# The front end of a streaming-encoder layer in another order, with its input projection as products of split halves

## What is computed

```python
h = layer_norm(x)                                   # input norm
proj = h @ w_in + b_in                              # 1024 -> 2304 columns, split into 8 parts
y_lru = rg_lru(lru_x, ...) * gelu(lru_gate)         # 512 + 512 columns
y_swa = sliding_window_gqa(sq, sk, sv, ...)         # 256 + 128 + 128 columns
y_sb  = stick_breaking(bq, bk, bv)                  # 256 + 256 + 256 columns, 4 heads
y = concat(group_rms(y_lru), group_rms(y_swa), group_rms(y_sb))
h = layer_norm(alpha * h + y @ w_out + b_out)
h = layer_norm(alpha * h + moe_ffn(h))              # top 4 of 32 experts
```

## Time and profile before

| | |
|---|---|
| median of 3 runs | 1484.73 us (1483.04 to 1486.56) |
| the profiled execution, its time | 1485.46 us |
| its span, first to last instruction | 1483.8 us |
| end of the front end in it | about 309 us |
| granted TensorE clock, mean | 0.989 |
| busy in the span: PE, DVE, ACT, POOL | 96%, 82%, 66%, 34% |
| busy in the first 309 us: PE, DVE, ACT, POOL | 284.2, 150.4, 111.3, 65.1 us |

### The profile page before, as it was taken

One profiled execution on the slowest core, in us unless ns is written; L12 is line 12 of the kernel. 1 busy time (PEld: TensorE's weight loads), 2 busy tenths in 40 slices (PEclk: granted clock), 3 DMA queues, 4 the chain that ended last, 5 costly groups with the idle time before them and its releaser, 6 DMA issues.

```text
span 1483.8 us, 20629 instructions
## 1 busy us (share of the span) xinstructions
PE 1430.4 (96%) x6623; PEld 1121.7 (76%) x6623; DVE 1215.0 (82%) x1002; ACT 975.9 (66%) x710; POOL 501.0 (34%) x309
## 2 busy tenths in 40 slices
PE   7999979998999999999999999999999999999994
PEld 3466548986888888888888888888888888888873
DVE  5533366476999999999999999999999999999985
ACT  2244660165777777777777777777777777777772
POOL 4200124152334333333334334444443333333101
PEclk9999999998999999999999999999999999999998
DMA  8221135469999999999999999999999999999933
GB/s 265 69 61 54 42 121 220 167 251 332 356 380 385 379 379 390 378 377 379 386 377 373 371 382 385 386 382 389 382 375 380 380 377 378 387 373 380 358 130 126
DMA packets 86311, 461.44 MB, mean 311 GB/s; under 512 B 11912, under 2 KB 26506, under 8 KB 37130
## 3 DMA queue, kind: packets, MB, share of 16 engines
q1 hardware_dynamic: 75190, 431.91, 74.0%
q0 software_dynamic: 9648, 26.49, 7.7%
q10 hardware_dynamic: 1444, 2.66, 0.7%
HBM read 443.92 MB, written 25.76 MB: 317 GB/s over the span
## 4 chain that ended last, share of the span: by engine, by line
PE 74%; DVE 1%; DMA 1%; POOL 1%; issue 1%; POOLq 0%; DVEq 0%; ACT 0%; ACTq 0%
PE banks L1737 69%; PE banks L1705 2%; PE banks L1711 2%; DMA acc_dram<-glu_lin 1%; PE banks L1769 1%; POOL sel L1436 1%; PE banks L1832 0%; POOLq L1438 0%; DVE raw L1666 0%; DVEq L1557 0%; DVE raw L1670 0%; PE banks L1699 0%; PE banks L1837 0%; DVE glu_lin L1553 0%; ACT hi L1324 0%
## 5 line engine op out<-in xcount | busy, mean ns | idle before, releaser
L1516 DVE TENSOR_TENSOR lo<-raw,hi 128x2048 fp32r<-128x2048 f32 x384 | 866.8, 2289 | 77.2 <-ACT hi L1324 76.3
L1324 ACT ACTIVATE hi<-raw 128x2048 fp32r<-128x2048 f32 x384 | 733.7, 1920 | 251.3 <-PE banks L1737 251.0
L1737 PE MATMUL banks<-hi,x_hi 128*128 128x512 f32 x1040 | 287.0, 397 | 9.3 <-DVE x_lo L1540 6.9
L1737 PE MATMUL banks<-lo,x_hi 128*128 128x512 f32 x1040 | 280.1, 391 | 0.0
L1737 PE MATMUL banks<-hi,x_lo 128*128 128x512 f32 x1040 | 279.7, 390 | 0.0
L1436 POOL TENSOR_SCALAR sel<-cst,rank_e 128x128 bf16<-128x128 f32 x120 | 219.4, 1840 | 126.8 <-issue 126.8
L1737 PEld LDWEIGHTS banks<-lo,x_hi 128*128 128x128 f32 x1040 | 195.8, 188 | 42.0
L1737 PEld LDWEIGHTS banks<-hi,x_hi 128*128 128x128 f32 x1040 | 191.1, 189 | 48.1 <-issue 11.7
L1737 PEld LDWEIGHTS banks<-hi,x_lo 128*128 128x128 f32 x1040 | 195.8, 188 | 41.6
L1459 POOL DMA_INDIRECT acc_dram<-ye,dst_row x31 | 50.2, 1620 | 363.5 <-ACT ye L1349 363.5
L1737 PE MATMUL banks<-hi,a_hi 128*128 128x512 f32 x496 | 155.7, 395 | 0.0
(11 more groups left out here) (276 smaller groups left out, 1226.1 us busy)
## 6 DMA issues: line engine op xcount, KB each, us to landing
raw<-in_w_exp_in SPq DMA_DIRECT2D x256, 1024.0 KB, 7.6
raw<-in_w_exp_out SPq DMA_DIRECT2D x128, 1024.0 KB, 6.7
raw<-in_w_in SPq DMA_DIRECT2D x9, 1024.0 KB, 7.9
raw<-in_w_out SPq DMA_DIRECT2D x4, 1024.0 KB, 5.0
x<-in_x SPq DMA_DIRECT2D x4, 512.0 KB, 6.0
h_dram<-x SPq DMA_DIRECT2D x4, 512.0 KB, 2.6
bias_in<-bias_dram SPq DMA_DIRECT2D x128, 3.0 KB
raw<-acc_dram SPq DMA_DIRECT2D x4, 512.0 KB, 5.9
```

What stands on the lines that cost most here:

```text
L1324: act.activation(hi[:, c0 % PARTS, :], raw[:, c0 % RAW, :], ACT.Copy).then_inc(hi_done, 1)
L1516: dve.tensor_tensor(lo[:, c0 % PARTS, :], raw[:, c0 % RAW, :], hi[:, c0 % PARTS, :].bitcast(F32), ALU.subtract).then_inc(lo_done, 1)
L1737: last = pe.matmul(psum[:, bank + n, :], s[:, k, :], w[:, at:at + 512], start=(first and m == 0 and new), stop=(closes and m == steps - 1 ...
```

## The change

Six things change, all in the front end.

1. The list starts with the stick-breaking heads: `bq`, `bk`, `bv` come first, the LRU's inputs later, the gates `g` and the window's score products later still. The norm of the stick-breaking group comes first (`NORM_ORDER = [2, 0, 1]`).
2. The input projection is three products of split halves instead of a plain float32 product. ACT makes the high half of the weights (`w_hi`, type float32r), DVE the low half (`w_lo`, the weights minus the high half), half a chunk at a time (`w_part`). The activations are split as well: ACT writes `hT_hi`, POOL subtracts the shift from it (`h_raw`), DVE makes `hT_lo` from the PSUM bank and that (`h_part`). A float32r product is one pass on PE, and there are three of them.
3. The two halves live where `raw` lies: `w_lo` over slots 0 and 1, `w_hi` over slots 2 and 3, so that only two chunks are held (`MIX_RAW = 2`). `hT_lo` lies over `x`, `hT_hi` over `h1T`, so the residual is no longer kept: x is loaded again once all input jobs are done, ACT normalises it (step `res`), and POOL applies gain, shift, alpha and the output bias.
4. `sv` is computed like the other jobs and transposed by a new job `u0`.
5. The window softmax is cut in two steps, `most` (maxima) and `window`; the small LRU constants become a step `lam`.
6. The output projection takes 512 columns at a time, and for the first token tile goes by the groups of channels, in the order of the norms; two of its products come early.

```diff
-WIN_ORDER = [0, 1, 6, 7, 8, 4, 5, 2, 3]
-MIX_RAW = 4
+WIN_ORDER = [6, 7, 8, 0, 1, 4, 5, 2, 3]
+MIX_SLOTS = 4
+MIX_RAW = 2
...
-STEPS = (jobs("x0") + [("rel", 0)] + jobs("x1", "x2", "x3", "bq0", "r0", "r1", "r2", "r3", "bq1")
-         + jobs("r4", "r5", "r6", "r7", "bk0", "bk1")
-         + [("z", 0)] + jobs("bv0") + [("lru", 0)] + jobs("bv1") + [("s", 0)] + jobs("sq0") + [("a", 0)]
-         + [("z", 1)] + jobs("sq1", "sk") + [("lru", 1), ("s", 1)] + jobs("sv") + [("a", 1)]
-         + [("z", 2)] + jobs("g0", "w0", "w1", "w2", "w3") + [("window", 0), ("s", 2)] + jobs("g1", "g2") + [("a", 2)]
-         + [("z", 3)] + jobs("g3", "t0", "t1", "t2", "t3") + [("lru", 2), ("squares", 0), ("s", 3)]
-         + jobs("q0", "v0", "v1", "v2", "v3") + [("norm", 0), ("squares", 1)] + jobs("q1") + [("a", 3), ("norm", 1)]
-         + [("squares", 2)] + jobs("q2") + [("norm", 2)])
+STEPS = (jobs("bq0") + [("rel", 0)] + jobs("bq1", "bk0") + [("z", 0)] + jobs("bk1", "bv0") + [("s", 0)] + jobs("bv1")
+         + [("a", 0)]
+         + [("z", 1)] + jobs("x0", "x1") + [("s", 1), ("lam", 0)] + jobs("x2") + [("a", 1)]
+         + [("z", 2)] + jobs("x3", "r0", "r1", "r2", "r3", "sq0") + [("s", 2)] + jobs("r4", "r5", "sq1", "r6", "r7")
+         + [("a", 2)]
+         + [("z", 3)] + jobs("sk", "w0", "w1", "w2", "w3") + [("most", 0)] + jobs("sv") + [("s", 3)] + jobs("u0") + [("lru", 0)]
+         + jobs("g0") + [("a", 3), ("window", 0)] + jobs("g1") + [("lru", 1)] + jobs("g2")
+         + [("squares", 2)] + jobs("q2", "t0", "t1", "t2", "t3") + [("norm", 2)] + jobs("g3", "v0", "v1", "v2", "v3")
+         + [("lru", 2), ("squares", 0)] + jobs("q0") + [("res", 0), ("squares", 1), ("early", 0), ("norm", 0)] + jobs("q1")
+         + [("norm", 1)])
...
+                sp.dma_start(gain_in, wide(t["ln_in_g"])).then_inc(wide_in, 16)
+                for i in range(NT):
+                    sp.dma_start(x[:, i, :], t["x"][P * i:P * i + P, :]).then_inc(x_back[i], 16)
+                sp.dma_start(shift_in, wide(t["ln_in_b"])).then_inc(wide_in, 16)
...
+                def w_part(u):
+                    g = u // 2
+                    act.wait_ge(mix_in[mixer_slot(g)], mixer_full(g))
+                    if g >= MIX_RAW:
+                        act.wait_ge(job_ready, DONE_WITH[g - MIX_RAW])
+                    act.activation(mixer_hi(g)[:, :, half_of(u)], mixer_raw(g)[:, :, half_of(u)],
+                                   ACT.Copy).then_inc(w_hi_done, 1)
...
                         job(n)
+                        if n in IN_ORDER and IN_ORDER.index(n) + 2 < len(IN_ORDER):
+                            w_part(IN_ORDER.index(n) + 2)
+                    elif what == "res":
+                        act.wait_ge(off0_ready, 1)
+                        for i in range(NT):
+                            act.wait_ge(x_back[i], 16)
+                            act.activation(x[:, i, :], x[:, i, :], ACT.Identity, scale=rstd0[:, i:i + 1],
+                                           bias=shift0[:, i:i + 1]).then_inc(x_again, 1)
...
+                for k in range(KD):
+                    pool.wait_ge(hT_copied, k + 1)
+                    pool.wait_ge(hT_ready, KD if k >= KD - 2 else k + 1)
+                    pool.tensor_scalar(h_raw[:, k, :], hT_hi[:, k, :].bitcast(F32), vec[:, V_LNB + k:V_LNB + k + 1], None,
+                                       ALU.subtract).then_inc(h_off, 1)
...
+                def h_part(k):
+                    dve.wait_ge(h_off, k + 1)
+                    dve.scalar_tensor_tensor(hT_lo[:, k, :], psum[:, k, :], vec[:, V_LNG + k:V_LNG + k + 1], h_raw[:, k, :],
+                                             ALU.mult, ALU.subtract).then_inc(hT_lo_ready, 1)
...
+                    if name[:2] == "bv":
+
+                        pe.wait_ge(w_lo_done, 2 * g + 2)
+                        for m in range(2):
+                            tile = slice(P * (2 * half + m), P * (2 * half + m) + P)
+                            o = bank[:, 256 * m:256 * m + 256]
+                            for h, w in ((hT_hi, high), (hT_hi, low), (hT_lo, high)):
+                                for k in range(KD):
+                                    pe.matmul(o, h[:, k, tile], w[:, k, :], start=(h is hT_hi and w is high and k == 0), stop=False)
+                            last = pe.matmul(o, ones[0:1, :], vrow[0:1, :], start=False, stop=True)
+                    else:
+                        own = half_of(u)
+                        for w, h, signal, done in ((high, hT_hi, hT_copied, w_hi_done), (low, hT_hi, None, w_lo_done),
+                                                   (high, hT_lo, hT_lo_ready, w_lo_done)):
+                            pe.wait_ge(done, u + 1)
```

More of the change, by code:

```diff
@@ L202, in hybrid_layer @@
         vec = sb("vec", [P, NVEC])
+        with ExitStack() as other:
+            w_lo = sb("w_lo", [P, MIX_RAW, CW], F32R, other)
+            w_hi = sb("w_hi", [P, MIX_RAW, CW], F32R, other)
         raw = sb("raw", [P, RAW, CW])
@@ L486, in job @@
                     elif name == "sv":
+                        last = act.activation(tmp[:, :], bank, ACT.Identity, bias=vec[:, V_BIN + 11:V_BIN + 12])
+                    elif name == "u0":
                         src = bank.rearrange("p (i j d) -> p i j d", i=NT, j=2)
@@ L608, in _ @@
                     if i:
+                        act.wait_ge(res_ready, NT)
                         act.wait_ge(h1T_ready, i)
@@ L767, in _ @@
                         last.then_inc(conv_ready, 1)
-                    elif what == "window":
+                    elif what == "most":
                         dve.wait_ge(band_in, 16 * 4)
@@ L787, in _ @@
                         last.then_inc(win_max, 1)
+                    elif what == "window":
                         dve.wait_ge(win_exp, 1)
@@ L971, in job @@
                         tiles = GROUPS[g][1]
-                        pe.wait_ge(y_sq, sum(len(GROUPS[i][1]) for i in range(g + 1)))
+                        pe.wait_ge(y_sq, normed_by(g))
                         for c in tiles:
```

262 lines of the change are left out of this document (157 added, 105 removed).

## The result

The changed kernel takes 1498.50 us (median of 4 runs, 1498.02 to 1499.05), the kernel before in the same session 1484.41 us (4 runs, 1483.04 to 1486.56). The ratio is 1.0094, with a 95% interval of 1.0076 to 1.0111: slower by 14.1 us. The profiled execution took 1498.23 us, beside the 1485.46 of before. It was predicted at 1498.1.

What follows compares the result with a forecast made beforehand. PE was taken to bound the front end, with slack on ACT and DVE. Saved work of -27.7 us plus waits of 6.0, 6.1, 5.6, 12.6 and 1 and clock 9 gave +12.6, about 1497 us; range 1483 to 1507.

Steps and rivals of the forecast that it cites:

- PE work, -27.7: Front end's input jobs, `sv` and `bv`: split one-pass products take 27.7 us of work off PE.
- The opening, +6.0: First job `bq0`: its last products wait for `hT_lo` behind POOL's eight subtractions, ending at 30.1; +6.0 us.
- The values, +6.1: Before head 0's value job: ACT and DVE chain of 11.6 us against 5.5 of PE work; +6.1 us.
- The keys, +5.6: Before `w0`: doubled window keys come 11.1 us after the scores, PE has `sk` for 5.5; +5.6 us.
- `q2`, +12.6: Stick-breaking norm: squares come after 30.3 us on ACT and 1.6 on DVE, PE has 19.3; +12.6 us.
- The other norms, +1: LRU group and group 1: PE waits some 9.7 us together, where it stood still 8.7 before; +1 us.
- The clock, +9: Behind five new front-end waits the granted clock may drop, each costing up to 3 us; four taken, +9 us.
- I look for no second effect.: Behind the front end: the change touches nothing there, so its gain or loss shifts everything one for one.
- A: Rival, front end: the clock stays up behind the new waits; sum +3.6, 1488.3 us; chance 15%.
- B: Rival, before `q2`: ACT is not the bound, deciding at a 22 us stretch; -3.0, 1481.7 us; chance 18%.
- C: Rival, first two layer norms: POOL's residual and DVE hold each other up, 18 us; +6 more, 1503; chance 15%.
- D: Rival: value products held by weight loads, +5.1, and chunks late, +5; 1507 us; chance 7%.

Runs made afterwards that it cites:

- e9: Changed kernel's heads-first order with e7's two edits, steps behind head 0 spread as in e8, one VectorE drain before the LRU's last product; 1461.66 us, 0.9843 of before.
- e10: Kernel before with its own float32 products and four slots, only its list of steps spread in the way of e8; 1480.63 us, 0.9975 of before.
- e7: e2 plus the transfer to `rel_dram` moved behind the exp of head 0; 1491.70 us, 1.0053 of before.
- e5: Changed kernel with dummy TensorE products put into its waits, as in e1 but cut to what the waits hold; 1494.44 us, 1.0069 of before.
- e12: e9 with dummy products in two waits, ahead of head 0's suffix sums and head 3's values; 1459.08 us, 0.9829 of before.
- e8: Changed kernel with e2's opening and a third order: LRU inputs first, gate and window products spread between input jobs; 1463.93 us, 0.9868 of before.
- e3: Changed kernel with its steps in the order of the kernel before, all else as changed; 1483.82 us, 0.9988 of before.
- e11: e8 with ScalarE's wait for the `rel_dram` write and the `band` loads moved from `lam` to the LRU's step; 1461.57 us, 0.9844 of before.
- e4: Changed kernel with job `g3` moved ahead of the squares of the stick-breaking group and of `q2`; 1497.93 us, 1.0105 of before.
- e6: Kernel before, unchanged, profiled once more for its second block; 1485.84 us, one run.
- e1: Changed kernel with dummy TensorE products put into its waits, which outlasted some of them; 1494.41 us, 1.0075 of before.
- e2: Changed kernel with half of GpSimd's eight opening subtractions moved to VectorE; 1495.72 us, 1.0082 of before.

## Why the prediction was right, and where it was not

The forecast of 1497 met 1498.5. None of its three signs of being wrong appeared: `q2` waited 12.08 us, the clock fell to 0.50, GpSimd's operation of 512 columns took 1.56. But the front end ended at 325.5 and not at some 321. By its own steps:

**PE work, -27.7.** Two jobs took from 87.80 to 99.08, 5.64 each for 5.49. A tile of `bv` took 3.67 for 3.45; a product of 256 columns 0.127 for 0.117 (24 in 3.04 us). The term should have been -24.6; the 23.7 us that PE is busy less in e9 than in e10 are close to it. A pass is not the same length in the two kinds, which is why three can be shorter than two: for 512 columns 0.43 us in the plain product (27.73 for 64 in the earlier trace rows) and 0.235 in the split one (5.64 for 24).

**The opening, +6.0.** The step was right and the size short: GpSimd's subtraction took 1.56 us, not 1.39, and `bq0` ended at 31.9, not 30.1. The half of an operation of 1024 columns was too low a price for one of 512. In the rows, with VectorE's first and last low half:

```profile
18.23 12.37 POOL L705 TENSOR_SCALAR x<-hT_hi,vec 128x512 f32<-128x512 f32 x8 [11.47 <-PE banks L1036]
...
19.93 0.75 DVE L767 SCALAR_TENSOR_TENSOR hT_lo<-banks,vec,x 128x512 fp32r<-128x512 f32 x1 [2.90 <-POOL x L705]
...
30.64 0.75 DVE L767 SCALAR_TENSOR_TENSOR hT_lo<-banks,vec,x 128x512 fp32r<-128x512 f32 x1 [0.79 <-POOL x L705]
```

**The values, +6.1.** Measured 7.71. The step that failed stood under "No cost expected": "a chunk of 1 MB is 3.7 us at the 281 GB/s of the earlier trace rows, and a start-up". The chunks took 5.5 us in the median, and the one that met the write to `rel_dram` 9.3, which e7 takes away. The cover that I named held for all the other chunks.

**The keys, +5.6, and `q2`, +12.6.** Measured 5.64 and 12.08. ScalarE's stretch went from 175.29 to 205.2, 29.9 us for the 30.3 of the walk. e9 shows that it is the stretch and not that the heads come first.

**The other norms, +1.** 3.38 and 6.37 are 9.75, for 9.7, and by the mechanism named: ScalarE's `res` began at 230.35, when the new x had come, some 14 us behind the end of `g3` for the 13 estimated, and took 4.97.

**The clock, +9.** The loss did rise by 9.0, from 3.0 to 12.0. But the step from a loss to a cost failed: "each can cost 3 us" was added up as if every loss came through whole. e5 took away 8.6 of it and gained 4.0; what is lost ahead of a wait that another engine ends is taken up by the wait. In e12 hardly such a wait was left, and 2.2 of 2.3 came through. On the other side the router's loss was 3.4 more than before, which the prediction did not have. From the router's products for the third token tile to the second block it is 23.8 us in the changed kernel and in e12 (loss 5.1), 21.1 before and 21.2 in e9 (1.7), and 20.0 in e8 (0.0): 2.7 of the 3.4 came through.

**The sum.** With the measured terms it is -24.6 + 7.8 + 7.7 + 5.6 + 12.1 + 1.0 for the waits, 4.4 for the clock (9.0 less the 4.6 that e5 shows to be taken up) and 2.7 in the router: +16.7, beside 16.3 measured at the second block. The front end was thus undersized by 3.7 us.

**"I look for no second effect."** This step failed. The stop of the earlier trace rows cost 1.6 us less and the last norm's wait, 3.55 before, was not there. In the profiled pair that gave 4.4 us back, so the total of +12.8 came out near 12.6 partly by luck, by two errors that cancel. Against the medians, +14.1, the forecast is 1.5 low.

**The rivals.** A fell: the clock did not stay up. B fell: the stretch is 29.9 us, and 22 was its point. C happened where it was named, in the first two layer norms, and cost nothing: beside GpSimd's residual operations VectorE's multiplications by gain and shift took up to 3.21 us each, 1.23 in the kernel before with GpSimd idle, some 7 us more in all where 18 were priced. PE had no wait over 0.33 us behind it, and from the first transposes for the router (265.88, before 252.13) to the second block it is 59.6 us for 57.0, which is the router's clock. DVE and POOL of the changed kernel:

```profile
256.67 3.21 DVE L936 TENSOR_TENSOR x<-x,affine 128x1024 f32<-128x1024 f32 x1
259.96 3.21 DVE L938 TENSOR_TENSOR x<-x,affine 128x1024 f32<-128x1024 f32 x1
```

```profile
258.77 3.32 POOL L738 TENSOR_TENSOR x<-x,h1T 128x1024 f32<-128x1024 f32 x1
262.23 3.15 POOL L740 TENSOR_TENSOR x<-x,h1T 128x1024 f32<-128x1024 f32 x1
```

And DVE before:

```profile
241.91 1.23 DVE L841 TENSOR_TENSOR x<-x,affine 128x1024 f32<-128x1024 f32 x1
```

In the opening, VectorE's low half, one input of which is in PSUM, took 0.75 us beside GpSimd's subtractions and also at 30.64, behind the last of them. That agrees with the Trainium skill, "SBUF — State Buffer", section "SBUF: two separate sides", for VectorE. GpSimd's 1.56 is its own time: the first subtraction, from 18.23, took it too, while VectorE stood idle until 19.93. D was partly right: the value products took 0.127, not the 0.17 of its upper bound, and one chunk came 3.8 us late.

## What to carry to other kernels

If work is taken from the engine that bounds a stretch, the others' chains must be compared anew with what now covers them: some 25 us of saved products, with what came with them, were worth nothing in the old list (e3), cost 14 in the new one, and gained 17 once the list was spread (e9 beside e10). Walk each engine's queue forward from the point that starts a chain to the one that waits for it, and count every operation that stands between them in that queue, whomever it serves; here that walk gave the waits before the keys, `q2`, `q0` and `q1` within some 0.5 us. Price a low clock only where the slow stretch ends in work of the same engine, not where it ends in a wait that another engine sets.

## What the runs showed of the hardware that I had not expected

In the router's stretch PE had no gap over 0.3 us, and yet the granted clock fell to 0.50, its lower level of 1.2 GHz. The same 16 products with the router's weights in the changed kernel, third and fourth token tile:

```profile
301.68 1.97 PE L1210 MATMUL banks<-w_rt,h1T 128*128 128x32 f32 x16 [0.28 <-ACT h1T L682]
...
306.53 3.46 PE L1210 MATMUL banks<-w_rt,h1T 128*128 128x32 f32 x16
```

The loss in the router came out as 0.0 us in e8 and e11, as 1.7 in before, e3, e4, e6, e7, e9 and e10, and as 5.1 in after, e1, e2, e5 and e12, with the same instructions: up to 5 us between kernels whose edits did not touch this stretch. What decides it is open; no run varied the router itself. The Trainium skill, in "TensorE: Matmul & The Clock Gate", section "Part 1: The HAM clock gate (the "warmup" mystery)", says that one kernel runs more or fewer of its first products at the low level from run to run. That is the climb at a kernel's start, and no run here shows it for the router: the one kernel that was profiled twice, before and e6, lost 1.7 us both times, though at places 5 us apart.

A write of 192 KB to `rel_dram` by 4 partitions took about 10 us and a 1 MB load issued 3.6 us behind it landed 3.9 us later than the same load without that write (9.3 for 5.4, e7); issued 2.0 us behind it, in e2, it took 10.8.
